# A norm made in two passes, latents first, and the projections behind it in another order: a two-block transformer kernel in float32 on one core

## The reference, cut to what matters

```python
# first block: x is 512 x 1024, h_ctx is 256 x 1024, m and mc are modulation rows
x = _residual(x, _swiglu(_modnorm(x, g[0], m[0], m[1]), ffn1_w1[l], ffn1_w3[l], ffn1_w2[l]),
              g[1], m[2], HALF_STEP)
h_ctx = _residual(h_ctx, _swiglu(_modnorm(h_ctx, g[0], mc[0], mc[1]), ffn1_w1[l], ffn1_w3[l], ffn1_w2[l]),
                  g[1], mc[2], HALF_STEP)
qa, ka, va, qn, qr, kn, kr, vb, ga, gb = _project(_modnorm(x, g[2], m[3], m[4]), *pw)
cqa, cka, cva, cqn, cqr, ckn, ckr, cvb, cga, cgb = _project(_modnorm(h_ctx, g[2], mc[3], mc[4]), *pw)
# neighbourhood attention, then low-rank attention, merge, second feed-forward

def _residual(x, y, g_post, gate, weight):
    return x + weight * gate * _rmsnorm(y, g_post)

# second block
h = rmsnorm(x, norm_mix_g[i])
proj = h @ w_in[i]     # convolved qk, v, o, gates, window attention q, k, v
qk_ml = jax.nn.silu(causal_depthwise_conv(qk_ml, conv_qk[i]))
...
x = x + jnp.square(jax.nn.relu(u)) @ w_down[i]
gate = jax.nn.sigmoid(rmsnorm(x, norm_ple_g[i]) @ w_ple_gate[i])
```

## Time and profile before

| | |
|---|---|
| time, median of 3 runs | 2944.09 us (2942.57 to 2946.95) |
| the profiled execution | 2944.31 us, of which the span from first to last instruction is 2942.5 us |
| PE busy | 2855.0 us (97%) |
| DVE busy | 1333.5 us (45%) |
| POOL busy | 798.2 us (27%) |
| ACT busy | 486.0 us (17%) |
| mean granted TensorE clock | 0.990 |

### The profile page before, as it was taken

The page is one execution under the profiler, slowest core; times in us unless marked ns, Lnnn a source line. Parts: engine busy times, 40 slices in busy tenths (PEclk is TensorE's granted clock), DMA queues, the critical chain, the costliest instruction groups (busy, mean ns, idle before and its releaser), DMA issues.

```text
span 2942.5 us, 29710 instructions
## 1 busy us (share of the span) xinstructions
PE 2855.0 (97%) x11820; PEld 2024.8 (69%) x11820; DVE 1333.5 (45%) x2453; ACT 486.0 (17%) x1040; POOL 798.2 (27%) x672
## 2 busy tenths in 40 slices
PE   8999999999999999999999998999989999999997
PEld 4655555555877377864888884776548865888873
DVE  7656565655127443324332335216545324544443
ACT  2100000012125143112000101005431001000011
POOL 1234343331222001421444430110014412544420
PEclk9999999999999999999999999999999999999999
DMA  6334333341110100221222221220002222222211
GB/s 240 118 111 136 100 114 114 93 145 43 58 30 9 51 1 30 86 97 53 86 86 86 87 85 57 72 74 15 29 34 92 89 81 72 93 91 87 86 51 64
DMA packets 51753, 231.66 MB, mean 79 GB/s; under 512 B 4256, under 2 KB 10784, under 8 KB 38176
## 3 DMA queue, kind: packets, MB, share of 16 engines
q1 hardware_dynamic: 40960, 181.17, 17.9%
q0 software_dynamic: 9072, 39.85, 4.3%
q10 hardware_dynamic: 1584, 8.75, 0.8%
HBM read 227.66 MB, written 2.10 MB: 78 GB/s over the span
## 4 chain that ended last, share of the span: by engine, by line
PE 91%; DVE 6%; ACT 1%; issue 1%; DMA 1%; POOL 0%; DVEq 0%; ACTq 0%
PE banks L630 60%; PE banks L568 19%; PE banks L753 2%; PE banks L776 2%; PE banks L986 1%; PE banks L901 1%; PE banks L994 1%; DVE scratch_b L1682 1%; PE banks L1156 1%; DVE banks L1990 1%; DVE rstd L1665 1%; PE banks L914 1%; DVE residual L1688 1%; PE banks L987 0%; DMA big<-w_ada 0%
## 5 line engine op out<-in xcount | busy, mean ns | idle before, releaser
L630 PE MATMUL banks<-big 128*128 128x256 f32 (+1 forms) x2256 | 576.0, 403 | 0.0
L2373 POOL TENSOR_TENSOR big<-weight_ring 128x512 f32<-128x512 f32 (+2 forms) x118 | 142.5, 1208 | 1465.4 <-PE banks L630 777.1
L630 PEld LDWEIGHTS banks<-big 128*128 128x128 f32 x2256 | 428.0, 190 | 113.2 <-DVE rpb_rows L1776 2.5
L630 PE MATMUL banks<-big,weight_ring 128*128 128x256 f32 (+1 forms) x1512 | 400.1, 409 | 3.3 <-DVE scratch_a L1782 2.6
L630 PE MATMUL banks<-normed,weight_ring 128*128 128x256 f32 (+1 forms) x1328 | 346.4, 404 | 2.1 <-ACT rstd L1598 1.3
L630 PEld LDWEIGHTS banks<-big,weight_ring 128*128 128x128 f32 x1512 | 286.8, 190 | 88.0 <-DVE scratch_a L1782 3.8
L630 PEld LDWEIGHTS banks<-normed,weight_ring 128*128 128x128 f32 x1328 | 252.2, 190 | 70.4 <-ACT rstd L1598 2.1
L568 PE MATMUL banks<-normed,weight_ring 128*128 128x512 f32 (+3 forms) x752 | 292.2, 547 | 6.8 <-ACT normed L1241 3.6
L568 PEld LDWEIGHTS banks<-normed,weight_ring 128*128 128x128 f32 (+2 forms) x752 | 140.8, 189 | 151.6 <-issue 140.9
L2374 POOL TENSOR_TENSOR big<-weight_ring 128x512 f32<-128x512 f32 (+2 forms) x143 | 212.8, 1488 | 0.0
L630 PE MATMUL banks<-normed,big 128*128 128x256 f32 (+1 forms) x848 | 205.6, 389 | 0.0
(11 more groups left out here) (424 smaller groups left out, 3423.7 us busy)
## 6 DMA issues: line engine op xcount, KB each, us to landing
weight_ring<-weights SPq DMA_DIRECT2D x144, 1024.0 KB, 4.8
rpb_rows<-w_ada POOLq DMA_DIRECT2D x28, 512.0 KB, 3.9
p_embed<-w_ada POOLq DMA_DIRECT2D x28, 512.0 KB, 3.9
weight_ring<-weights SPq DMA_DIRECT2D x16, 768.0 KB, 4.3
weight_ring<-weights SPq DMA_DIRECT2D x14, 512.0 KB, 3.3
weight_ring<-weights SPq DMA_DIRECT2D x8, 640.0 KB, 3.7
big<-w_ada POOLq DMA_DIRECT2D x2, 2048.0 KB, 8.4
residual<-xT ACTq DMA_DIRECT2D x2, 1536.0 KB, 12.2
```

The source lines that it names most:

```text
L630: last = nc.tensor.matmul(z, stationary(p), moving(p), start=opens and p == 0, stop=p == kp - 1, skip_group_check=True)
L2373: T(w[2], a11, a21, ALU.subtract).then_inc(sums_c, 1)
```

## The change

The norm ahead of the projections is done twice over, for the latents first (`na`, `LAT`) and then for the context (`na_context`, the same semaphores counted on by `base=KC, turn=1`). PE's sums for the context stand between query tiles 1 and 2. The fast units follow in the order 6, 7, 8, 4, 5, 2, 3, 9, and the weights are streamed so. The addition of the squares at the ends of the three feed-forwards moves from behind a fast unit into it. In the second block the wait for the convolution moves from value tile 0 to value tile 4, and the value tiles take other PSUM banks.

```diff
-    ("proj", "proj", 0, 10, UNIT), ("kr", "kr", 0, 1, KC * QK_D), ("uq", "uq", 0, 4, 2 * QR * QK_D),
+    ("proja", "proj", 0, 2, UNIT), ("projb", "proj", 6, 3, UNIT),
+    ("projc", "proj", 4, 2, UNIT), ("projd", "proj", 2, 2, UNIT), ("proje", "proj", 9, 1, UNIT), ("kr", "kr", 0, 1, KC * QK_D), ("uq", "uq", 0, 4, 2 * QR * QK_D),
...
-PROJ_FAST = range(2, 10)
+PROJ_FAST = (6, 7, 8, 4, 5, 2, 3, 9)
...
+        na_context = dict(na, base=KC, turn=1)
...
-            return (z, z + 1, z + 2, 3 - z, 6, 7, 4 - z, 5 - z)[b] if b < 8 else (6, 7, z, z + 1)[b - 16]
+            return (6, 7, 4, 5, 0, 1, 2, 3)[b] if b < 8 else (6, 7, z, z + 1)[b - 16]
...
+                pe.wait_ge(g["added"], 2 * g["turn"] + 2)
+                pe.wait_ge(ada["done"], 2 * N_MOD * KC)
+                total(SQA1, 0, 6, True)
+                total(SQA1, 1, 7, True)
+                pe.wait_ge(g["done"], 4 * g["turn"] + 4)
+                total(SQB1, 0, 6, False).then_inc(g["used"], 1)
+                total(SQB1, 1, 7, False).then_inc(g["used"], 1)
...
-            turn_over(18, cst, 0, 2 * P)
-            norm_sums(na, BOTH)
-            turn_over(14, cst, 0, 2 * P)
+            turn_over(13, cst, 0, 2 * P)
+            norm_sums(na, LAT)
+            turn_over(12, cst, 0, 2 * P)
             for b in range(4):
+                if b == 2:
+                    norm_sums(na_context, CONTEXT, (5,))
...
             def contexts(b, v):
-                if b >= 4:
-                    pe.wait_ge(proj["act"], 2 + contexts_upto(b - 2))
+                if contexts_upto(b) > 2:
+                    pe.wait_ge(proj["act"], contexts_upto(b))
+                else:
+                    pe.wait_ge(na["ready"], 2 * KC)
...
-            pe.wait_ge(conv["mixed"], 8)
-
-
             for b in PROJ2:
+                if b == 4:
+                    pe.wait_ge(conv["mixed"], 8)
                 if b == 16:
                     for m, v in enumerate(V_QSW):
                         if m < 2:
-                            pe.wait_ge(prj2["act"], 2 + 2 * m)
-                            pe.wait_ge(prj2["dve"], 2 + 2 * m)
+                            pe.wait_ge(prj2["act"], 4)
+                            pe.wait_ge(prj2["dve"], 3 + m)
...
             act.wait_ge(sq1["used"], 1)
-            root(na, BOTH, (6, 7), na["y_root"], D)
-            norm_squares(na, T, 2)
-            norm(na, BOTH, 3)
+            root(na, LAT, (6,), na["y_root"], D)
+            act.wait_ge(sq1["used"], 2)
+            root(na, CONTEXT, (7,), na["y_root"], D)
+            norm_squares(na, LAT)
+            norm(na, LAT, 3)
+            norm_squares(na_context, CONTEXT)
+            norm(na_context, CONTEXT, 3, (5,))
...
-            def add_squares(g, m, a=SQA, b=SQB):
-                dve.wait_ge(g["done"], 4 * g["turn"] + m + 1)
-                V.tensor_tensor(a, a, b, ALU.add).then_inc(g["added"], 1)
+            def squares_within(g, m, a, b):
+
+                def add():
+                    dve.wait_ge(g["done"], 4 * g["turn"] + m)
+                    V.tensor_tensor(a, a, b, ALU.add).then_inc(g["added"], 1)
+                return [lambda: None, add] if m >= 2 else None
...
-            post_norm(na, BOTH, GATE1)
-            norm(na, BOTH, modulated(SCALE2), True)
-
-
-            dve.wait_ge(na["ready"], 2 * KC)
+            for g, parts in ((na, LAT), (na_context, CONTEXT)):
+                post_norm(g, parts, GATE1)
+                norm(g, parts, modulated(SCALE2), True)
+
+
+            dve.wait_ge(na["ready"], KC)
+            dve.wait_ge(na["scaled"], 2 * KC)
             row_sums_of(8, H, lambda i: [(0, 2), (2, 2)] if i in (1, 3) else [(0, 4)], (2, 0, 1, 3))
```

More of the change, by code:

```diff
@@ L203 @@
 BOTH = [(0, S, 0), (S, T, 1)]
+CONTEXT = [(S, T, 1)]
 NA_S = (0, 1, 6, 7)
@@ L486, in contexts_upto @@
         def contexts_upto(b):
-            return sum(1 for c in range(2, b + 1) if with_context(c))
+            return sum(1 for c in PROJ_FAST[0:PROJ_FAST.index(b) + 1] if with_context(c))
         PROJ2 = (*range(8), *range(16, 20))
@@ L697, in squares_of_both, with total @@
             def squares_of_both(g):
-                for rows, first in ((SQA1, True), (SQB1, False)):
-                    if first:
-                        pe.wait_ge(g["added"], 2 * g["turn"] + 2)
-                        pe.wait_ge(ada["done"], 2 * N_MOD * KC)
-                    else:
-                        pe.wait_ge(g["done"], 4 * g["turn"] + 4)
-                    for k in range(2):
-                        for (a, b, _), q in zip(BOTH, (6, 7)):
-                            last = nc.tensor.matmul(bank[:, q, 0:b - a], ones, rows[:, k * T + a:k * T + b],
-                                                    start=first and k == 0, stop=not first and k == 1)
-                last.then_inc(g["used"], 1)
+                def total(rows, part, at, first):
+                    a, b, _ = BOTH[part]
+                    for k in range(2):
+                        last = nc.tensor.matmul(bank[:, at, 0:b - a], ones, rows[:, k * T + a:k * T + b],
+                                                start=first and k == 0, stop=not first and k == 1)
+                    return last
+                pe.wait_ge(g["added"], 2 * g["turn"] + 2)
[5 more added lines that the diff above has]
+                total(SQB1, 1, 7, False).then_inc(g["used"], 1)
             def added_sums(g, parts, banks, added):
@@ L848, in _ @@
                 v = V_PROJ[b]
-                if b == 3:
+                if b == PROJ_FAST[0]:
+                    pe.wait_ge(na["root"], 2)
+                if b == PROJ_FAST[1]:
                     pe.wait_ge(proj["act"], 2)
                     pe.wait_ge(proj["dve"], 2)
-                fast(v, H, 8, TOTALS_P if b == 2 else None, None, (lambda: contexts(b, v)) if with_context(b) else None)
+                fast(v, H, 8, TOTALS_P if b == PROJ_FAST[0] else None, None, (lambda: contexts(b, v)) if with_context(b) else None)
             n = SEQ["kr"]
@@ L1218, in _, with norm_squares @@
             act.dma_start(CS[:, 1, :], cB[:, 1, :]).then_inc(ada["c_ctx_landed"], 16)
-            def norm_squares(g, width, per_chunk):
+            def norm_squares(g, parts):
+                (a, b, _), = parts
                 for k in range(KC):
-                    if per_chunk:
-                        act.wait_ge(g["xnew"], g["base"] + per_chunk * (k + 1))
+                    act.wait_ge(g["xnew"], g["base"] + k + 1)
                     if k >= 2:
                         act.wait_ge(g["sq_used"], g["base"] + k - 1)
-                    A(SQ[:, k % 2, 0:width], X[:, k, 0:width], ACT.Square).then_inc(g["sq"], 1)
+                    A(SQ[:, k % 2, a:b], X[:, k, a:b], ACT.Square).then_inc(g["sq"], 1)
             def root(g, parts, banks, signal, features):
@@ L1231, in root, with norm @@
                     A(rs[:, a:b], bank[:, n, 0:b - a], ACT.Sqrt, bias=eps, scale=1.0 / features).then_inc(signal, 1)
-            def norm(g, parts, shift):
+            def norm(g, parts, shift, banks=(6, 5)):
                 act.wait_ge(g["sq_used"], g["base"] + KC)
-                root(g, parts, (6, 5), g["root"], D)
+                root(g, parts, banks, g["root"], D)
                 if shift is not None:
@@ L1626, in _ @@
             last_down(V_DOWN3[3][0], X, sq3)
-            act.wait_ge(sq3["used"], 3)
+            act.wait_ge(sq3["used"], 4)
             root(nple, LAT, (6,), nple["root"], D)
@@ L1663, in norm @@
                 dve.wait_ge(g["root"], g["turn"] + len(parts))
-                width = parts[-1][1]
-                link(V.reciprocal(rs[:, 0:width], rs[:, 0:width]))
+                lo, hi = parts[0][0], parts[-1][1]
+                link(V.reciprocal(rs[:, lo:hi], rs[:, lo:hi]))
                 for k in range(KC):
@@ L1671, in post_norm @@
             def post_norm(g, parts, gate_row):
-                dve.wait_ge(g["y_root"], len(parts))
-                width = parts[-1][1]
-                link(V.reciprocal(rs[:, 0:width], rs[:, 0:width]))
+                dve.wait_ge(g["y_root"], g["turn"] + len(parts))
+                lo, hi = parts[0][0], parts[-1][1]
+                link(V.reciprocal(rs[:, lo:hi], rs[:, lo:hi]))
                 marks = {}
```

47 lines of the change are left out of this document (22 added, 25 removed).

## The result

The changed kernel takes 2926.49 us (median of five runs, 2924.57 to 2928.32), the kernel before 2944.05 on the same chip (five runs, 2942.41 to 2946.95). The ratio is 0.9943, with a 95% interval of 0.9933 to 0.9954: about 17 us less. The forecast was 2927.5. The profiled execution took 2924.57 us for a span of 2922.7, so 19.8 us less span than the profiled one before.

The account below looks back on a forecast made before the run. PE holds 91% of the chain, DVE carrying it before the first query tile. First norm and projections 8.3, convolution's wait 5.2, squares 3.3: 16.8 us off 2944.3 gives 2927.5; own range 2925 to 2930, over the cases 2921.5 to 2933.

Parts of the forecast that it names:

- Step 1: First norm: the latents' root comes earlier, with squares added inside the fast unit; reciprocal at 655.4, 4.0 us earlier.
- A: Stage: first feed-forward's last square to reciprocal; rival: GpSimd's weight sums don't disturb the chunks, 2923.5 us, chance 0.18.
- Steps 2 and 3: First norm: latents' pass 10.6 us shorter, but GpSimd's weight sums meet DVE's chunk operations, costing 4.0 us.
- B: Stage: first norm's reciprocal to first query tile; rival: context late on PE, costing 6 to 8; 2930.5 us, chance 0.20.
- Steps 4 and 6: Context's sums in PE's stream between query tiles 1 and 2 cost 4.3 us; query tiles at speed gain 2.0.
- C: Stage: first query tile to first attention's reciprocal; rival: the convolution's wait only moves to query-unit copies, 2932.7 us, chance 0.05.
- Step 5: Row sums behind the context's second reciprocal cost zero, with 1 to 4 us of cover before the first fast unit.
- Step 7: Projections: the other order of the fast units, their contexts and the ring of weights is worth zero.
- Step 8: Value tiles: the convolution's wait of 3.2 us goes and the tiles take 2.0 us less, 5.2 together.
- Step 9: Ends of second and third feed-forwards: PE's waits for the addition of squares shrink by 1.6 and 1.7 us.
- D: Stage: first attention's reciprocal to second feed-forward's; rival: most of first norm's gain is eaten, about 2939 us, chance 0.04.
- E: Stage: first convolved tile to second block's first query unit; rival: slower, PE longer at 1.2 GHz, 2965 us, chance 0.03.

Follow-up runs that it names:

- two passes, first group held: Two passes and new order, squares still added behind the fast unit, with GpSimd's first weight sums held until the latents' eight chunks are done: A 6.24, B 22.2 us.
- old order: Changed kernel with the projections' fast units back in the order 2 to 9: C 662.12 us in both.
- the kernel with spread sums: Changed kernel with the context's eight sums of squares spread over query tile 2, one ahead of each chunk: C 2.0 us longer, PE waits 1.4 us.

## Why the prediction was right

*Step 1, forecast 4.0, measured 3.6* (A, 8.30 to 4.71), 3.9 in the kernels where the residual landed sooner. The bound by root and landing was right. The working took the 7.14 us of before as the old order's cost, though part of it was the low clock. At full clock the old order has an A of 6.24 (two passes, first group held), so the order itself is worth 1.5 to 1.9 us; the other 1.7 is that PE no longer sums at 1.2 GHz there, as in all ten traces with the new order. It also took the last square to start as before; it comes 0.3 us earlier, a gain that no step counted.

*Steps 2 and 3, forecast 10.6 - 4.0 = 6.6, measured 6.9* (B). The two terms were tried apart: the undisturbed pass is 22.23 us (22.24 forecast), the collision 3.7 (4.0), of which 3.3 is DVE and 0.4 PE's clock in the sums behind it. The turns were priced at 1.06 us per DVE operation; the four operations lost 3.3 us together, single ones up to 1.06. My worry over the 477 ns row was for nothing: SCALAR_TENSOR_TENSOR is hit like the other. The Trainium skill, SBUF — State Buffer, section SBUF: two separate sides, says that the engine that starts first holds the shared pair of ports for its whole instruction and the other blocks, and that of DVE's plain operations those with two SBUF inputs are concerned, against a GpSimd operation that reads SBUF. The trace agrees: 1.74 against 0.68 for two inputs, while the reciprocal of 768 columns, with one input, takes 4.96 us in the kernel before both beside GpSimd's operations and, at 685.18, without them.

*Steps 4 and 6, forecast -4.3 + 2.0 = -2.3, measured -2.8* (C). The context's sums took 4.66 in the chain, since a pair of them goes by in 1.27 us and not 1.1; that leaves 1.8 for the query tiles. Without the turn-over matmuls the tiles take 2.2 more, so this gain needs them. They don't explain it alone: the kernel before had 14 of them ahead of its query tiles and was still granted 0.56 there. How the 1.8 divides between the clock and the chunks that arrive faster was not tried.

*Step 5, forecast 0 with 1 to 4 us of cover*: no wait, and 4.6 us of cover. Row sums 4.8 us later, for a unit 1.2 us earlier, made a wait of 1.4.

*Step 7, forecast 0*: 0 (old order).

*Step 8, forecast 5.2*: 5.15, alone and in the whole. Of it 3.4 is up to the first value tile and 1.8 within the tiles. The 3.4 is the wait. The 1.8 is the clock behind it (0.57 in the first 4 us before), and it doesn't always come: the kernel with the addition of squares alone has the same wait, was granted 1.00 behind it, and its value tiles lost only 0.1 us. Of the four traces with the wait, three had the fall; of the ten without it, none. That kernel's chain of waits (57.21 before):

```profile
1857.83 55.52 PE banks L568 x256
```

*Step 9, forecast 1.6 + 1.7*: 1.8 + 1.8.

The sum is 16.8 against 16.3 for the steps that it counts, and holds nearly term by term. That the median lies only 1.0 us from the forecast is partly luck: five executions of the changed kernel lie up to 3.8 us apart. The places in the trace that the prediction named as signs are off by the 2.1 us up to the last square; counted from that square, the first query tile starts after 30.6 us, where 30.5 was forecast. The rivals A, B and C were each met by a run and fell; D and E by the result.

## What to carry over

An operation that comes earlier can land beside another engine's work that it used to miss: the root came 3.6 us earlier, the collision cost 3.7, and only with GpSimd's sums held back, a wait of one line on work that even then ends some 35 us ahead of the first fast unit, were both gains there. Where DVE carries the chain, look in the timeline for GpSimd beside its two-input operations, and count a full turn for each. And read such a change by stages between fixed pieces of work: here a ratio of medians couldn't tell 2 us, while C, D and E agree to 0.1 in kernel after kernel. Look at the granted clock before a difference between stages is put down to the edit: of the 2.0 us by which C is longer in the kernel with spread sums, 1.6 are clock and 0.4 the edit.

## What the hardware showed that I had not expected

A turn costs by the instruction and not by its size: 256-column operations on DVE went from 0.42 to 1.49 us and from 0.48 to 1.37, 512-column ones from 0.68 to 1.74 and from 0.75 to 1.64. For their length, small operations suffer most.

The same stretch of unchanged code is granted the clock differently from one kernel's execution to the next, where PE idles ahead of it: 0.91 or 1.00 in the start phase (1.7 us), 7.12 or 5.43 us for the same sixteen sums, 3.5 or 2.0 us for the last four, value tiles of 57.2 us before and 55.5 in the kernel with the squares alone, though the same wait stands ahead of both, and the first attention 1.5 us longer in two traces of fourteen. Each is worth 1 to 2 us. They add up to more than most single steps of this change. What decides it wasn't tried, and it need not be chance everywhere: the last four sums took 3.4 to 3.5 us in the three traces of kernels with neither the new addition of squares nor the moved wait for the convolution, and 2.0 to 2.9 in all others, so part of that 1.5 us may come from the change after all.
